# Where the gemm's streamed tiles start in SBUF, against the loaded ones

## The reference

```python
h = rmsnorm(x, g_pre) * (1 + scale) + shift            # 256 x 1024
z, xbc, dt, q, kv, nsa_gate, z_att, merge_gate = split(h @ w_in)
y_ssm = mamba2_branch(z, xbc, dt, ...) @ w_ssm_out     # 2048 -> 1024
y_nsa = nsa_branch(q, kv, nsa_gate, z_att, ...) @ w_nsa_out
merged = sig(mg0) * y_ssm + sig(mg1) * y_nsa
return x + gate * rmsnorm(merged @ w_out, g_post)
```

## The kernel before, in words

| tensors | role in the gemm | start before | mod 512 | start after | mod 512 |
|---|---|---|---|---|---|
| `h_hi`, `h_lo` (and `o_hi`, `o_lo` in the same place) | moving | 16,832 | 448 | 16,960 | 64 |
| `w_raw` | source of the split | 33,216 | 448 | 33,344 | 64 |
| `w_hi`, `w_lo` | stationary | 53,888 | 128 | 53,888 | 128 |
| `ynorm_hi`, `ynorm_lo` (and `merged_hi`, `merged_lo`, stationary in the output projection) | moving | 101,312 | 448 | 100,928 | 64 |
| all that lies behind `z_at`: attention and SSM work tiles, `q_hi_lo`, `k_hi`, `k_lo` | both | | 448 | 384 bytes lower | 64 |

## Time and profile before

### The profile page before, as it was taken

The page is one execution under the profiler, slowest core; times in us unless marked ns, Lnnn a source line. Parts: engine busy times, 40 slices in busy tenths (PEclk is TensorE's granted clock), DMA queues, the critical chain, the costliest instruction groups (busy, mean ns, idle before and its releaser), DMA issues.

```text
span 490.6 us, 9766 instructions
## 1 busy us (share of the span) xinstructions
PE 448.6 (91%) x3592; PEld 409.9 (84%) x3592; DVE 350.1 (71%) x611; ACT 267.8 (55%) x518; POOL 232.7 (47%) x238
## 2 busy tenths in 40 slices
PE   0759989999999989997879899999999999999995
PEld 0439989999999879996779889888999898999874
DVE  0167989598999989888867986846565766549643
ACT  1354776555585585735485674555746564445441
POOL 0043453458476847985353563244444543335340
PEclk9987998999999999999999998999999999999999
DMA  8976444633435235326856782325243333356402
GB/s 307 425 298 228 160 138 154 190 122 130 174 124 173 91 112 190 114 104 229 328 184 246 265 294 87 126 89 173 92 134 123 132 126 130 130 180 222 156 2 86
DMA packets 21959, 82.99 MB, mean 169 GB/s; under 512 B 2444, under 2 KB 2834, under 8 KB 20626
## 3 DMA queue, kind: packets, MB, share of 16 engines
q1 hardware_dynamic: 21912, 82.37, 47.6%
HBM read 81.31 MB, written 1.05 MB: 168 GB/s over the span
## 4 chain that ended last, share of the span: by engine, by line
PE 67%; issue 8%; POOL 7%; DMA 7%; DVE 5%; ACT 4%; SPq 1%; DVEq 0%; POOLq 0%; ACTq 0%
PE gemm L617 17%; PE gemm L618 16%; PE gemm L619 16%; DMA w_raw<-in_wpack 7%; PE y_or_o L814 2%; ACT w_hi L843 2%; POOL cmp_blocks L459 2%; POOL w_lo L1412 1%; PE y_or_o L696 1%; PE score L778 1%; PE score L780 1%; SPq L472 1%; DVE w_lo L1092 1%; PE small L564 1%; PE small L566 1%
## 5 line engine op out<-in xcount | busy, mean ns | idle before, releaser
L1412 POOL TENSOR_TENSOR w_lo<-w_raw,w_hi 128x256 fp32r<-128x256 f32 (+1 forms) x117 | 133.6, 1147 | 173.5 <-ACT w_hi L843 167.8
L617 PE MATMUL gemm<-h_hi,w_hi 128*128 128x256 f32 x680 | 198.9, 293 | 4.5 <-DVE w_lo L1092 2.3
L618 PE MATMUL gemm<-h_lo,w_hi 128*128 128x256 f32 x680 | 192.9, 284 | 0.0
L619 PE MATMUL gemm<-h_hi,w_lo 128*128 128x256 f32 x680 | 192.5, 283 | 0.0
L1092 DVE TENSOR_TENSOR w_lo<-w_raw,w_hi 128x768 fp32r<-128x768 f32 (+1 forms) x117 | 128.2, 1098 | 58.8 <-ACT w_hi L843 58.6
L843 ACT CAST w_hi<-w_raw 128x1024 fp32r<-128x1024 f32 x117 | 122.1, 1045 | 45.7 <-PE gemm L619 27.9
L617 PEld LDWEIGHTS gemm<-h_hi,w_hi 128*128 128x128 f32 x680 | 130.8, 192 | 8.3 <-issue 7.3
L618 PEld LDWEIGHTS gemm<-h_lo,w_hi 128*128 128x128 f32 x680 | 130.9, 193 | 0.6
L619 PEld LDWEIGHTS gemm<-h_hi,w_lo 128*128 128x128 f32 x680 | 130.5, 192 | 0.0
L1141 DVE SCALAR_TENSOR_TENSOR conv_acc<-gemm,conv_half,conv_acc 128x255 f32<-128x255 f32 (+2 forms) x72 | 34.5, 480 | 8.2 <-ACT conv_acc L877 6.2
L617 PE MATMUL gemm<-ynorm_hi,w_hi 128*128 128x256 f32 x128 | 36.5, 285 | 0.0
(11 more groups left out here) (233 smaller groups left out, 780.0 us busy)
## 6 DMA issues: line engine op xcount, KB each, us to landing
w_raw<-in_wpack SPq DMA_DIRECT2D x133, 512.0 KB, 3.4
w_ada_shift_scale<-in_w_ada SPq DMA_DIRECT2D x8, 1024.0 KB, 15.1
x_T<-in_xT SPq DMA_DIRECT2D x1, 1024.0 KB, 10.6
x_residual<-in_x_tok SPq DMA_DIRECT2D x1, 1024.0 KB, 7.9
out_tok_dram<-out_tok SPq DMA_DIRECT2D x4, 256.0 KB, 2.1
consts<-in_consts SPq DMA_DIRECT2D x1, 272.0 KB, 22.6
cmp_bias_and_valid<-in_cmp_bias SPq DMA_DIRECT2D x1, 272.0 KB, 6.1
w_compress<-in_w_compress SPq DMA_DIRECT2D x1, 192.0 KB, 5.5
```

The source lines that it names most:

```text
L617: nc.tensor.matmul(bank[:, 0:SEQ], w_hi, hi[:, k0 + k, :], start=first, stop=False)
L618: nc.tensor.matmul(bank[:, 0:SEQ], w_hi, lo[:, k0 + k, :], start=False, stop=False)
L619: last = nc.tensor.matmul(bank[:, 0:SEQ], w_lo, hi[:, k0 + k, :], start=False, stop=end)
L1412: nc.gpsimd.tensor_tensor(WL[:, n % LO_SLOTS, c:1024], RAW[:, u % RAW_SLOTS, c:1024], WH[:, n % HI_SLOTS, c:1024], ALU.subtract).then_inc( ...
```

## The change

Three places of padding are replaced by a function `home`, which moves the address cursor on to a given remainder mod 512. The small tensor `softmax_small` goes in front of `h_hi`. No instruction is added, taken away or put elsewhere; only addresses change.

```diff
+LINES = 512
+MOVING, LOADED = 64, 128
...
+    def home(remainder):
+
+        cursor[0] += (remainder - cursor[0]) % LINES
+        return cursor[0]
+
     MOD = place("mod", [P, 16], f32)
     EPSC = place("eps_columns", [P, 3], f32)
     AB = place("ada_scale", [P, 16], f32)
     GG = place("gate_times_g", [P, 2, 8], f32)
-    cursor[0] += 64
-    h_at = cursor[0]
+    SM = place("softmax_small", [P, 2, 4, 4], f32)
+    h_at = home(MOVING)
     HH = place("h_hi", [P, KT, SEQ], f32r)
     HL = place("h_lo", [P, KT, SEQ], f32r)
     RAW = place("w_raw", [P, RAW_SLOTS, 1024], f32)
-    SM = place("softmax_small", [P, 2, 4, 4], f32)
-    cursor[0] += 64
+    home(LOADED)
     WH = place("w_hi", [P, HI_SLOTS, 1024], f32r)
     WL = place("w_lo", [P, LO_SLOTS, 1024], f32r)
...
-    cursor[0] = ys_at + 8192 + 384
+    cursor[0] = ys_at + 8192
     YS = place("y_ssm_out", [P, 8, SEQ], f32, at=ys_at)
-    z_at = cursor[0]
+    z_at = home(MOVING)
     Z = place("z_gate_then_y", [P, 16, SEQ], f32)
     YNH = place("ynorm_hi", [P, 16, SEQ], f32r, at=z_at)
     YNL = place("ynorm_lo", [P, 16, SEQ], f32r)
```

## The result

| | before | after |
|---|---|---|
| median of 15 runs each | 493.51 us (491.51 to 496.50) | 490.85 us (488.58 to 496.68) |
| ratio after / before | | 0.9949, 95% interval 0.9926 to 0.9972 |
| a second comparison, 12 runs of the changed kernel | 493.65 us | 490.64 us, ratio 0.9949 (0.9919 to 0.9979) |
| profiled execution, own time and span | 492.43, 490.6 us | 493.53, 491.7 us |
| mean granted clock, all timed executions | 0.9806 (108) | 0.9751 (27) |

The change makes the kernel about 2.5 us faster, 0.5%, where 6.8 us were forecast. The ratios leave out executions over 1.5% above the fastest of their kernel, of which three on record lie far out (742 us for `e2_z_only`, 2473 us before, 2495 us for `e9_keep_busy`). The pitch of the gemm did fall, and nearly to the value forecast.

What follows compares the result with a forecast made beforehand. The prediction took TensorE, through the pitch of the gemm's matmuls, to bound the kernel. The profiled 492.4 us less 6.8 us gave 485.6, and 1.2 us more for the median gave 486.8 us; range 479 to 498 us.

Steps and rivals of the forecast that it cites:

- The mechanism: Gemm's moving tiles: at 64 short instead of 192, stream and weight load never meet; 4 ns a matmul saved.
- The load's 111.5 ns: Gemm's weight load, taken as the floor under the 117.9 ns pitch, 6.4 ns below it.
- Rival 1: Gemm pitch: place doesn't matter, the stream itself is limited to some 8.7 B/ns; time stays at 493.6 us; chance 0.36.
- the conversion into time: Gemm matmuls counted by stretch, 1696 together, at 4 ns each: 6.8 us saved.
- the shares: 1230 gemm matmuls counted fully, half of 60-90 and 300-330 us (182), a third of 150-300 us (284).
- The edits costed at nothing: Output projection, DVE and POOL split, tensors behind `z_at`: 0 taken; possible 0.5 us either way, 2 us loss, 1 us either way.
- Rival 2: Gemm slower because the two starts come nearer to equal: about 122 ns a matmul, 500 to 504 us; chance 0.21.
- the three cases: Whole kernel: the forecast (479 to 491 us) 0.43, no effect (491.1 to 496.1) 0.36, slower 0.21.
- the first case: Gemm pitch falls and the kernel is faster by over 0.5%, 479 to 491 us; chance 0.43.
- the second: No effect on the kernel: 493.6 us, 491.1 to 496.1; chance 0.36.

Runs made afterwards that it cites:

- e2_z_only: The kernel before with only `z_at` moved to a remainder of 64 (`ynorm` 64 short, `h` and `o` still 192 short): 491.63 us, ratio 0.9965.
- e9_keep_busy: The changed kernel with 20 and 14 bfloat16 matmuls added ahead of two steps to keep TensorE at work in waits: 492.26 us, ratio 0.9973.
- the short table: Bare gemm matmuls on zeroed operands, no layer computed, with shorter loads or other column counts: 512 columns take 233.3 ns at 64 short, 228.9 at 192.

## Why the prediction was half right

**The mechanism** held: the pitch of the gemm fell, and the medians of the large groups on the other engines stayed (a few small ones moved, the longest on DVE `ynorm_lo` from 567 to 833 ns, 16 of them, and on POOL `cb_decay` from 1583 to 1412, 8 of them). The value taken, 113.9 ns (4 ns less), is close to the mean that the stretches bound by TensorE have now, 114.5; the short pattern's 113.3 is a little below both. The reason given for it was only partly right. That load and stream hinder each other, and by their distance, is shown (6.7 ns at 0 short, gone with a short load). That they meet once and pass each other, so that 64 short is a gap in which they never meet, is not: 192 short, where they meet by that working, has the short pattern too, 144 short is better than 64, and the period is 256 bytes and not 512. The load's 111.5 ns was the wrong floor; the one that is reached is 113.3, which a shorter load doesn't lower. The floor of 111.5 was measured with one streamed column, and the supposition was marked as shown by no row; that the pitch fell to near the forecast owes something to luck.

**Rival 1** was right in one half: a floor exists that a shorter load doesn't lower (17/16 of one column a cycle at full clock), but it lies at 113.3 ns, and before the change the gemm stood 4.4 ns above it. The first rule of the Trainium skill quoted there ("SBUF — State Buffer", § Who interferes with whom) doesn't hold in these runs: the same matmul took 0 to 6.7 ns longer according to where its two operands lie, with no other engine at work.

**The step that failed is the conversion into time**, "4 x 1696 = 6.8 us": its 4 ns was too much (3.2 came), and it put the change of the granted clock at nothing without a reason (about 5.4 us more at half clock came, worth 1.2 to 2.3 us). Its third part, the shares, isn't settled.

1. *The pitch.* 4 ns was taken for all; a mean of 3.2 ns came in the bound units (117.7 to 114.5), because about a quarter of the matmuls there (a third of all) stay in the long pattern. Over the 1230 matmuls counted in full this is 3.9 us and not 4.9, and the bound units measure 4.0.
2. *The shares.* A third of the matmuls from 150 to 300 us and a half of two other windows, together 466, were counted at 4 ns: 1.9 us. The runs don't settle these shares. Over the nine traces below, units 40 to 70 show 0.05 us for each ns of mean pitch, give or take 0.2, where a third would be 0.24 and the whole 0.72: not the whole, but nothing and a third both fit. Work added in the stretch cost some 0.4 of itself when spread over it, with the clock's part taken off, and all of itself when put in a lump at 200 us.
3. *The clock.* The prediction had nothing on it. The mean granted clock is 0.9751 in the changed kernel and 0.9806 before; at half the rate for the time in question, the difference is 0.0055 x 2 x 490 = 5.4 us more at half clock in an execution. In the nine traces of kernels with no added work, units 40 to 70 take about 129 us plus 0.43 us for each us at half clock (from 129.9 with 3.4 to 136.5 with 17.1), and over 14 of the 15 executions of the changed kernel (without the longest) the time rises by 2.3 us for each 0.01 that the clock is lower; over the 108 of before it is 2.1. By the one the 5.4 us cost 2.3 us, by the others 1.2. With the 4.0 us won in the bound units alone that leaves 1.7 to 2.8 us, where 2.5 to 2.7 are measured; with all 1696 matmuls at 3.2 ns, 5.4 us, it leaves 3.1 to 4.2. So the clock takes some of the gain back, and the shares are likelier near nothing than as counted; how much falls to each is argued from these correlations, since all three experiments that raised the clock paid for it with work of their own. It stays open.

What the traces do show of its cause: TensorE reaches the sixth `y` step 2.2 us sooner (178.8 for 181.1 us), POOL's instruction lets it go only 0.7 us sooner (182.7 for 183.4), the wait is 3.9 us for 2.3, and half clock goes with it, in both traces of the changed kernel and not in the one before. But the faster pitch isn't shown to be what lengthens the wait. The kernel with an equal start has a slower pitch than before (119.8 ns), and its timeline and windows have this:

```profile
184.26 0.51 PE L702 MATMUL y_or_o<-cb_decay,x_dt 128*64 128x128 f32 x5 [3.45 <-POOL cb_decay_across L1487]
...
184.00:188.00 4.00, 3.74 (x43) 3.60 (x44) 3.97 (x5) 0.53 (x2) 4.00 (x5) 1.00 0.33 120
```

Its wait is long too, and no half clock goes with it. All eleven traces of kernels with `h` and `w_raw` at new places have a wait of 3.2 to 3.9 us there, whatever their pitch, and eight of them 3.4 or 6.8 us at half clock with it; the kernel before and `e2_z_only`, with both at their old places, have 2.3 us and none. The mean granted clock, too, was 0.974 to 0.979 for all kernels with the new places and no added work, those with a slower pitch than before among them (0.979 and 0.978), and 0.979 to 0.981 in the five series of before. So the long wait goes with the new places and not with the pitch, and the lower clock seems to; why is open.

**The edits costed at nothing** cost nothing in durations, though the longer wait goes with the new places of `h` and `w_raw` taken together: the split's medians didn't move, the output projection's mean pitch is 232.2 ns (233.3 before; the short table has 233.3 and 228.9 for 512 columns at its two distances), and each half of the change alone gave what was expected of it. **Rival 2** would have been right in its sign for another distance: with an equal start the kernel is 0.8% slower. **The chances** gave the three cases 0.43, 0.36 and 0.21; what came is a pitch of the first case with a time at the edge of the second.

## What to carry to other kernels

A change that speeds up the engine on the path by n ns an instruction is worth close to n times the instructions in those stretches in which that engine has next to no idle time (4.0 us here, of 4.4 by the mean pitch); what it is worth elsewhere was below what these runs can tell. Adding work to the engine in such a stretch is a cheap way to ask, if two things are read beside the time: whether the granted clock moved, and whether the added work ran where it was meant to, which it didn't in two runs here. Where TensorE streams float32r at full clock, the places of the two operands mod 256 are worth a table of their own (113.3 to 120.0 ns for the same matmul), and the table has to be taken at the very places of the kernel. New addresses alone can move an engine's waits and TensorE's granted clock, so a forecast of a gain in pitch needs a term for the clock, even if only as a range.

## What the runs showed of the hardware

- A float32r matmul of 256 columns with a full load of its own repeats every 113.3, 116.7 to 119.8, or 120.0 ns at full clock, by the places of its operands in SBUF; the table repeats after 256 bytes of distance. At half clock it is 213.3 ns, as one column a cycle.
- At some places there are two steady patterns (113.3 and 117.8 ns) for the same instructions and addresses. At 64 short a series mostly keeps the one it falls into within six matmuls; at 144 short (weights at 64) it goes over to the short one within about a dozen.
- With a load of 32 columns it is still 113.3 ns (116.7 at 192 short). With 512 streamed columns it is 226.7 ns at 0 short, 233.3 at 64 and 228.9 at 192. 113.3 and 226.7 are 17/16 of one column a cycle. With 128 streamed columns and a full load it is 111.7 ns at all three distances tried.
- A shift of both operands by 16 bytes changed the pitch at the same distance from 113.3 to 120.0 ns.
